# A half-sum on GpSimd ahead of VectorE's sum over one-hot products

## The chip, the cores and the metric

The kernel runs on one core of one Trainium2 chip. The metric is the device time of one execution in microseconds (us), lower is better. Times shown as a median are over separate runs; the profile is one further execution with the hardware profiler on.

## What is computed

One inference step of a decoder layer over 1024 prompt tokens and 64 sample tokens (8 sequences of 8), 1024 channels, all in float32. Two token mixers in parallel (retention and a gated linear recurrence) are merged and projected by `w_out`; behind them stands PEER, an expert retrieval by product keys, which is the part that matters here:

```python
q = (xf @ w_q).reshape(T, 8, 256)
s1 = einsum('thd,nd->thn', q[..., :128], k1)      # 128 scores each
s2 = einsum('thd,nd->thn', q[..., 128:], k2)
v1, i1 = top_k(s1, 16); v2, i2 = top_k(s2, 16)
cand = v1[..., :, None] + v2[..., None, :]        # 256 sums
sc, pidx = top_k(cand, 16)
expert = e1 * 128 + e2                            # of the 16 picks
act = gelu(einsum('td,tkd->tk', x, u_tab[expert]))
out = einsum('tk,tkd->td', softmax(sc) * act, v_tab[expert])
```

Each token has 8 heads of 16 picks: 128 rows of `u_tab`, each of 1024 numbers, are gathered and multiplied with the token.

## The kernel before, in words

**Tiles and units.** Tokens stand in 9 tiles of 128 (the last one is half full, and is turned so that 128 partitions hold its picks). A unit `m` is one head of a pair of tiles: 32 units of two tiles, then 4 units of one tile for the samples, 36 in all. VectorE makes a unit's picks in 16 pieces (`piece`, lines 1458 to 1530): the top 16 of each score row with `max`, `max_index` and `match_replace` (lines 1479 to 1487), 54 candidate sums (`pairs`, only those 54 of the 256 can be in the top 16), their top 16 with positions `bp` (lines 1497 to 1519), and the ids of the 54 candidates, `cid`. Piece 15 then compares an iota of 54 with each of the 16 positions (line 1528): `hot[128, tile, 16, 54]` has one 1 in each group of 54, and signals `pos_ready`.

**From positions to ids.** GpSimd multiplies `hot` with the 54 ids (`products`, line 1346), one instruction for each tile, and counts `hot_ready`. VectorE sums each group of 54 (`ids`, line 1438), which leaves the one id that was picked, and turns it into an integer (line 1440) for the gathers; `ids(m - 1)` is called in piece 8 of unit m, so half a unit later.

**The gathers and the dots.** GpSimd issues one indirect DMA for each of 1088 columns (`gather`, line 1354): 128 rows of `u_tab`, 512 KB, into one of six buffers (`rows`, `VD` = 6). Gather n waits until dot n - 6 is done (`used`). VectorE's `dot` (line 1540) waits for the landing, multiplies the 128 rows with the tokens and sums, one instruction and a short accumulator read. The products of a unit are put between gathers by `product_at`: behind gather `done[m] + 7` and `done[m] + 9` in most cases, where `done[m]` is the column at which piece 15 of unit m is done. On GpSimd's queue everything is in this one order.

**The last stage.** From 1639 us on the work goes by quarters (numbered -2 to 13, 32 batches each). In a batch VectorE builds a one-hot of the picks (line 1601) and its product with the weights in three bfloat16 parts (`oh1w`, line 1605), then does its pieces and two dots, laid out by `steps` from a table written by hand (`stages`). TensorE turns `oh1w` into expert weights W with 12 short matmuls (line 2016), and from quarter 0 on multiplies one block of the value table with W for each batch (line 2029, 16 instructions a batch, the float32 matmul being two). VectorE may run two batches ahead of TensorE. The value table streams in through four buffers (`vbuf`) on SyncE's queue beside the gathers. At the end of every fourth quarter VectorE adds the accumulators to the residual (`finish`, line 1619).

`Chain` (`gl_` for GpSimd) lets an instruction count a semaphore and has its own engine wait for that count before it goes on.

Of the kernel before, what the change touches and what calls it, by code (L numbers as in the profile page):

```python
# [23 lines left out]
ALU = mybir.AluOpType  # L24
ACT = mybir.ActivationFunctionType
AX = mybir.AxisListType.X

P = 128
# [16 lines left out]
TOPK = 16  # L45
# [8 lines left out]
NCAND = 54  # L54
# [142 lines left out]
def program(nc, I, O, S):  # L197
# [3 lines left out]
    def sem(name):  # L201
        return ctx.enter_context(nc.semaphore(name))

    def sb(c, name, shape, dt=F32):
        return c.enter_context(nc.sbuf_tensor(name, shape, dt))

    def bc(ap, axis, shape):
        return ap.unsqueeze(axis).broadcast_to(shape)
# [14 lines left out]
    def hold(eng):  # L223

        eng.sem_inc(hold_sem, 1)

    with ctx:
# [10 lines left out]
        gl_ = Chain(nc.gpsimd, pool_chain)  # L238
# [38 lines left out]
        cand, cid = sb(ctx, "cand", [P, 2, NCAND]), sb(ctx, "cid", [P, 2, NCAND])  # L277
        bp, bpf = sb(ctx, "bp", [P, 2, TOPK], U32), sb(ctx, "bpf", [P, 2, TOPK])
        hot = sb(ctx, "hot", [P, 2, TOPK, NCAND])
        eidf = sb(ctx, "eidf", [P, 2, TOPK])  # L280
# [95 lines left out]
        with nc.Block() as block:  # L376
            @block.sync
            def _(sp):
                def ada_load(i):
                    s = EARLY[i]  # L380
                    sp.dma_start(ada[i][:, :, :], I["w_ada"][:, s * ADA_W:(s + 1) * ADA_W].rearrange("(k p) n -> p k n", p=P)).then_inc(ada_in[i], 16)
                for dst, src in ((cT, "cT"), (vec, "vec"), (bada, "bada"), (ident, "ident")):
                    sp.dma_start(dst[:], I[src]).then_inc(small_in, 16)
                sp.dma_start(hnA[:, :, 0:TA], I["xT"][:, 0:TA].rearrange("(k p) t -> p k t", p=P)).then_inc(x_in[0], 16)
                ada_load(0)
                ada_load(1)
                sp.dma_start(hnB, I["xT"][:, TA:T].rearrange("(k p) t -> p k t", p=P)).then_inc(x_in[1], 16)
                ada_load(2)
                ada_load(3)
                w_in_load(sp, 0, 0)  # L390
                sp.wait_ge(ones_ready, 4)
                wab_load(sp, 0)
                for j in range(1, 6):
                    w_in_load(sp, 0, j)
                sp.wait_ge(act_done, 1)
                for dst, src in ((rope_c, "rope_c"), (rope_s, "rope_s"), (dmask, "dmask"), (smask, "smask"), (xi, "xi"),
                                 (zeta, "zeta"), (szeta, "szeta"), (gch, "gch"), (h0, "h0"), (c0, "c0"), (iota, "iota")):
                    sp.dma_start(dst[:], I[src]).then_inc(small_in, 16)
                s0_load(sp, 0)
                sp.wait_ge(mod_ps, len(EARLY))  # L400
                slab_load(sp, 0)
# [794 lines left out]
        tk, dk, pos_ready, hot_ready, idx_ready, max_ready, exp_ready = (sem(n) for n in ("tk", "dk", "pos_ready", "hot_ready", "idx_ready", "max_ready", "exp_ready"))  # L1196
# [16 lines left out]
        def unit(m):  # L1213

            if m < NGRP * H:
                return m // H, m % H, 2
            return NGRP, m - NGRP * H, 1

        def spilled(m):
            return m - H  # L1220

        def scored(m):

            return m if m < H else H + m - NGRP * H if m >= NGRP * H else m + NSU
# [18 lines left out]
        with nc.Block() as block:  # L1243
# [97 lines left out]
            @block.gpsimd  # L1341
            def _(g):
                def products(m, t):

                    g.wait_ge(pos_ready, m + 1)
                    g.tensor_tensor(hot[:, t, :, :], hot[:, t, :, :], bc(cid[:, t, :], 1, [P, TOPK, NCAND]), ALU.mult).then_inc(hot_ready, 1)  # L1346

                def gather(n, table, t, col):

                    s = n % VD  # L1350
                    if n >= VD:
                        g.wait_ge(used, n - VD + 1)
                    hold(g)
                    g.indirect_dma_start(rows[:, s, :], None, table[:, :], bass.IndirectOffsetOnAxis(ap=eidx[:, (t // 2) % 2, t % 2, col:col + 1], axis=0)).then_inc(landed[s], 16)  # L1354
                def reload(m):

                    j, n = spilled(m), unit(m)[2] * PW
                    if j >= 2:
                        g.wait_ge(tk, (m - 2) * TKU + 10)
                    at = scored(m) - H  # L1360
                    g.wait_ge(sp_out[at % 2], 16 * (at // 2 + 1))
                    g.dma_start(scr[:, m % 2, 0:n], S["sc"][j][:, 0:n]).then_inc(sc_in[m % 2], 16)

                def reload_at(m):

                    j = spilled(m)
                    return 2 * P - 1 if j < 2 else min(read[m - 2] + 8, done[m - 1] + 1)

                def product_at(m, x):

                    G, h, _ = unit(m)
                    at = min(done[m] + VD + 1 + 2 * x, read[m + 1] + VD - 2 if m + 1 < NUNIT else NU - 1)
                    return min(at, G * GT + h * TOPK - 1)
                for t in range(2):
                    products(0, t)
                for n in range(NU):
                    t = n // P
                    if n % TOPK == 0 and t % 2 == 0:
                        g.wait_ge(idx_ready, (t // 2) * H + (n % P) // TOPK + 1)
                    gather(n, I["peer_u"], t, n % P)  # L1380
                    for m in range(1, NUNIT):
                        if m + 1 >= H and m + 1 < NUNIT and n == reload_at(m + 1):
                            reload(m + 1)
                        for x in range(unit(m)[2]):
                            if n == product_at(m, x):
                                products(m, x)
                for n in range(NU, NU + TS):
                    gather(n, I["peer_v"], NT - 1, n - NU)

            @block.vector  # L1390
            def _(v):
# [42 lines left out]
                def ids(m):  # L1434

                    G, h, nt = unit(m)
                    v.wait_ge(hot_ready, 2 * m + 2 if m < NGRP * H else NGRP * H + m + 1)
                    v.tensor_reduce(eidf[:, 0:nt, :], hot[:, 0:nt, :, :], AX, ALU.add).then_inc(dk, 1)  # L1438
                    v.wait_ge(dk, m + 1)
                    v.tensor_copy(eidx[:, G % 2, 0:nt, h * TOPK:(h + 1) * TOPK], eidf[:, 0:nt, :]).then_inc(idx_ready, 1)  # L1440

# [16 lines left out]
                def piece(x):  # L1458
# [7 lines left out]
                    if p < 10:  # L1466
# [5 lines left out]
                        if p == 8 and m and m != H:  # L1472
                            ids(m - 1)
# [177 lines left out]
                for half in range(2):  # L1651
                    if half:
                        ids(H - 1)
                    slots = steps(plan[2 + half])
                    for f in range(half * H // 2, (half + 1) * H // 2):
                        mix_vector(v, zB, f, lambda: mixed_step(next(slots)))
# [16 lines left out]
                for row in plan[7:]:  # L1673
                    i = row[0]
                    g, q = divmod(i, 4)
                    quarter(row)
                    if i >= 0 and q == 3:
                        finish(g)
                    if i == 10:
                        ids(NUNIT - 1)  # L1680
                    if i == 11:
                        soft_high(NGRP)
                        tile_weights(NT - 1, TS).then_inc(ef_ready, 1)
                        v.wait_ge(ef_ready, NT)
                    if i == 12:
                        dl_(v.tensor_tensor(sel, ident[:, 0:TS], ident[:, TS:P], ALU.add))
                        v.wait_ge(used, NU + TS)
                        v.sem_inc(acc_ready, 1)
                    if i >= 0 and i < 12 and q == 0:
                        soft_high(g + 1)  # L1690
                        tile_picks(2 * g + 2)
                    if i >= 0 and i < 12 and q == 2:
                        tile_picks(2 * g + 3)
                        if g:
                            norm(g - 1)
# [488 lines left out]
```

## Time and profile before

| | |
|---|---|
| time, median of 3 runs | 4003.32 us (4001.05 to 4008.05) |
| profiled execution: its time | 3999.14 us |
| profiled execution: its span | 3997.3 us (1.84 us lie around it) |
| busy: TensorE, VectorE, ScalarE, GpSimd | 3684.9, 2830.9, 1557.9, 1603.1 us |
| granted TensorE clock, mean | 0.971 of full speed |
| chain that ended last, by engine | PE 36%, DVE 28%, DMA 9%, issue 7% |

PE is TensorE, DVE is VectorE, ACT is ScalarE and POOL is GpSimd. A duration in a row of groups is the mean of one instruction; in a row by source it is min/median/max in ns. An idle time in square brackets stands in front of the instruction and names what ended it. A record's length holds the time in which the instruction was started but could not go on.

### The profile page before, as it was taken

The numbers are of one execution on the slowest core, as the hardware profiler recorded it, in microseconds if no ns is written. First come the engines' busy times: TensorE is split into PE (matmuls) and PEld (weight loads), VectorE is DVE, ScalarE is ACT, GpSimd is POOL, SyncE is SP. The second block draws the span as 40 slices with busy tenths as digits, with TensorE's granted clock in tenths as the row PEclk, the third lists the DMA queues.
The fourth block names the chain that finished last, engine by engine and source line by source line (L and its number), as shares of the span: only waits on it lengthen the run. The fifth ranks groups of instructions, "written<-read, shape, count | busy, mean of one in ns | idle before, by whom it ended". The sixth has DMA issues, their size and how long they took to land.

```text
span 3997.3 us, 65568 instructions
## 1 busy us (share of the span) xinstructions
PE 3684.9 (92%) x21008; PEld 2903.7 (73%) x21008; DVE 2830.9 (71%) x6544; ACT 1557.9 (39%) x3678; POOL 1603.1 (40%) x1252
## 2 busy tenths in 40 slices
PE   7999969999999988878899899999899999899998
PEld 4665656666656657767787788888788887788887
DVE  3333427588877767889899999999998898683000
ACT  3222211111112211676555455555555655465200
POOL 0000003243233324435666566666667776471000
PEclk9999989999999989999999999999999999999999
DMA  7343334565466578778999999999999999995443
GB/s 236 106 124 103 100 133 153 154 188 181 162 199 202 175 244 290 260 242 319 389 374 371 330 398 375 372 385 396 360 374 390 398 406 352 371 381 189 140 159 126
DMA packets 415882, 1060.14 MB, mean 265 GB/s; under 512 B 39665, under 2 KB 171121, under 8 KB 415729
## 3 DMA queue, kind: packets, MB, share of 16 engines
q0 software_dynamic: 168000, 610.87, 41.5%
q1 hardware_dynamic: 242672, 437.10, 31.1%
q10 hardware_dynamic: 5056, 10.49, 0.7%
q8 instruction: 52, 0.85, 0.1%
q14 instruction: 102, 0.83, 0.1%
HBM read 1031.70 MB, written 26.62 MB: 265 GB/s over the span
## 4 chain that ended last, share of the span: by engine, by line
PE 36%; DVE 28%; DMA 9%; issue 7%; POOL 2%; PEld 1%; ACT 0%; DVEq 0%; ACTq 0%; SPq 0%; PEldq 0%; POOLq 0%
DVE rows L1540 16%; PE vacc L2029 13%; PE vacc L783 10%; DMA rows<-in_peer_u,eidx 7%; PE vacc L752 4%; PE scat L1963 3%; DVE oh L1601 2%; POOL rows L1354 2%; DVE oh1w L1605 1%; DMA vbuf<-in_peer_v 1%; DVE eidf L1438 1%; PEld vacc L2029 1%; DVE hot L1528 1%; PE scat L2016 1%; PE vacc L606 1%
## 5 line engine op out<-in xcount | busy, mean ns | idle before, releaser
L2029 PE MATMUL vacc<-W,vbuf 128*128 (+1 forms) x8192 | 1900.4, 387 | 27.1 <-DMA vbuf<-in_peer_v 18.2
L1354 POOL DMA_INDIRECT rows<-in_peer_u,eidx x1088 | 1362.7, 1252 | 1270.4 <-DVE dots L1540 874.1
L2029 PEld LDWEIGHTS vacc<-W,vbuf 128*128 128x128 f32 x8192 | 1537.2, 192 | 224.4 <-issue 26.6
L1540 DVE CUSTOM_DVE_ANT_0 rows<-rows,htok 128x1024 f32<-128x1024 f32 x1088 | 1349.0, 1265 | 75.3 <-DMA rows<-in_peer_u,eidx 66.9
L1794 ACT ACTIVATE dist<-iota,e2s 128x128 bf16<-128x128 f32 x2048 | 648.6, 391 | 18.0 <-DVE wpart L1579 15.7
L1801 ACT ACTIVATE W<-scat 128x256 f32 x448 | 171.6, 383 | 813.4 <-PE scat L2016 806.1
L783 PE MATMUL vacc<-W 128*128 128x384 f32 x1280 | 431.3, 491 | 3.5 <-PE vacc L783 2.3
L1346 POOL TENSOR_TENSOR hot<-hot,cid 128x864 f32<-128x864 f32 x68 | 133.4, 1965 | 668.6 <-DVE hot L1528 667.4
L1797 ACT ACTIVATE oh<-dist,ones 128x512 bf16<-128x512 bf16 x512 | 369.6, 722 | 16.7
L783 PEld LDWEIGHTS vacc<-W 128*128 128x128 f32 x1280 | 240.0, 191 | 168.8 <-issue 10.7
L2016 PEld LDWEIGHTS scat<-oh1w,oh 128*128 128x128 bf16 x5376 | 217.9, 97 | 127.2 <-issue 69.7
L1605 DVE TENSOR_TENSOR oh1w<-oh,wpart 128x768 bf16<-128x768 bf16 x512 | 287.8, 562 | 17.7
L2016 PE MATMUL scat<-oh1w,oh 128*128 128x64 bf16 x5376 | 234.0, 192 | 50.3 <-DVE oh1w L1605 46.7
L1601 DVE TENSOR_TENSOR oh<-iota,e1s 128x256 bf16<-128x256 bf16 x512 | 165.4, 323 | 134.2 <-PE scat L2016 122.3
L1963 PE MATMUL scat<-W 128*128 128x256 f32 (+1 forms) x1024 | 250.4, 400 | 10.4 <-DVE W L1423 8.2
L1963 PEld LDWEIGHTS scat<-W 128*128 128x128 f32 x1024 | 195.0, 195 | 49.6 <-issue 9.7
L783 PE MATMUL vacc<-rows,W 128*128 128x320 f32 x640 | 181.9, 437 | 4.9 <-ACTq L683 2.5
L752 PE MATMUL vacc<-W 128*128 128x256 f32 x768 | 170.3, 382 | 2.8 <-PE vacc L793 2.8
L219 ACT ACTIVATE W<-vacc 128x768 f32<-128x768 f32 x32 | 25.9, 810 | 374.5 <-PE vacc L783 374.5
L752 PEld LDWEIGHTS vacc<-W 128*128 128x128 f32 x768 | 146.4, 191 | 28.4 <-issue 7.1
L783 PEld LDWEIGHTS vacc<-rows,W 128*128 128x128 f32 x640 | 118.4, 190 | 57.4 <-issue 7.8
L1354 POOL DMA_INDIRECT rows<-in_peer_v,eidx x64 | 90.1, 1408 | 42.2 <-DVE htok L1549 21.7
(300 smaller groups left out, 2913.5 us busy)
## 6 DMA issues: line engine op xcount, KB each, us to landing
vbuf<-in_peer_v SPq DMA_DIRECT2D x512, 512.0 KB
W<-in_w_in SPq DMA_DIRECT2D x80, 512.0 KB, 5.5
W<-in_wq SPq DMA_DIRECT2D x64, 512.0 KB, 4.7
vbuf<-in_w_ada SPq DMA_DIRECT2D x9, 2048.0 KB, 8.0
rows<-in_peer_u,eidx POOLq DMA_INDIRECT x1088, 7.9
W<-in_w_in SPq DMA_DIRECT2D x16, 1024.0 KB, 5.6
W<-in_w_out SPq DMA_DIRECT2D x2, 4096.0 KB, 19.8
W<-in_w_ada SPq DMA_DIRECT2D x3, 2048.0 KB, 16.1
```

What stands on the lines that cost most here:

```text
L752: mm = pe.matmul(dst, z.hnT[:, k, t * P:(t + 1) * P], w_qkv[:, k, :], start=(k == 0), stop=(k == KC - 1))
L783: mm = pe.matmul(pslice(z, pj if bank == "pj" else pk, s), w_part[j - 1][:, k, :], z.hnT[:, k, lo:hi], start=(k == 0), stop=(k == KC - 1))
L1354: g.indirect_dma_start(rows[:, s, :], None, table[:, :], bass.IndirectOffsetOnAxis(ap=eidx[:, (t // 2) % 2, t % 2, col:col + 1], axis=0)). ...
L1540: v.tensor_tensor_reduce(rows[:, s, :], rows[:, s, :], htok[:, t % 2, :], 1.0, 0.0, ALU.mult, ALU.add, dots[t % 3][:, c:c + 1]).then_inc(u ...
L1601: v.tensor_tensor(oh1[:, h, :, :, :], bc(iota4[:, half * HK:(half + 1) * HK, :], 1, shp), bc(e1s[:, k].rearrange("p (a n) -> p a n", n=2), ...
L1605: v.tensor_tensor(oh1w[:, h, :, :, :, :], bc(oh1[:, h, :, :, :], 1, shp), bc(wpart[:, u * QB + j, :, :, :], 3, shp), ALU.mult).then_inc(oh ...
L1794: ins = act.activation(dist[:, n, :], iota[:, :], ACT.Abs, bias=e2s[:, bass.ds(k, 1)], scale=-1.0)
L1797: act.activation(oh2[:, h, :, :], dist[:, :, :], ACT.Relu, bias=ones[:, 0:1], scale=-1.0).then_inc(oh2_ready, 1)
L1801: act.activation(W[:, half * HK:(half + 1) * HK, bass.ds(i * (VB * SB) + (u * P + q * SB), SB)], banks[q % 2][:, 0:SB * HK].rearrange("p ( ...
L1963: mm = pe.matmul(scat[u][:, 0:n], wq[j % 4][:, k, :], hn2T[g][:, k, 0:n], start=(k == 0), stop=(k == KC - 1))
L2016: mm = pe.matmul(banks[h][:, n * HK:(n + 1) * HK], oh2[:, h, n, :], oh1w[:, h, j, n // 2, :, n % 2], start=(j == 0), stop=(j == 2), skip_g ...
L2029: mm = pe.matmul(vacc[:, k, :], vbuf[:, s, k * P:(k + 1) * P], W[:, e1, :].rearrange("p o t -> p (o t)"), start=(clear and s == 0 and k % ...
```

## The change

`products` adds a second instruction on GpSimd: after the multiplication (now followed by a wait of GpSimd for its own result) the upper 27 of each 54 products are added onto the lower 27. VectorE's sum reads only those 27 of each group. `hot_ready` counts once for each tile as before.

```diff
@@ products (GpSimd)
                     g.wait_ge(pos_ready, m + 1)
-                    g.tensor_tensor(hot[:, t, :, :], hot[:, t, :, :], bc(cid[:, t, :], 1, [P, TOPK, NCAND]), ALU.mult).then_inc(hot_ready, 1)
+                    half = NCAND // 2
+                    gl_(g.tensor_tensor(hot[:, t, :, :], hot[:, t, :, :], bc(cid[:, t, :], 1, [P, TOPK, NCAND]), ALU.mult))
+                    g.tensor_tensor(hot[:, t, :, 0:half], hot[:, t, :, 0:half], hot[:, t, :, half:], ALU.add).then_inc(hot_ready, 1)
@@ ids (VectorE)
                     v.wait_ge(hot_ready, 2 * m + 2 if m < NGRP * H else NGRP * H + m + 1)
-                    v.tensor_reduce(eidf[:, 0:nt, :], hot[:, 0:nt, :, :], AX, ALU.add).then_inc(dk, 1)
+                    v.tensor_reduce(eidf[:, 0:nt, :], hot[:, 0:nt, :, 0:NCAND // 2], AX, ALU.add).then_inc(dk, 1)
```

## Rows read from the trace of the kernel before

**Rows 1.** The page's first part: busy time, share of the span, instructions.
```profile
PE 3684.9 (92%) x21008; PEld 2903.7 (73%) x21008; DVE 2830.9 (71%) x6544; ACT 1557.9 (39%) x3678; POOL 1603.1 (40%) x1252
```

**Rows 2.** Busy time by stretch: start:end, length, engines, clock, DMA share, GB/s.
```profile
1639.00:1997.00 358.00, 294.43 (x2346) 253.85 (x2347) 324.57 (x862) 242.48 (x644) 187.98 (x148) 0.98 0.86 309
1997.00:2961.00 964.00, 900.06 (x6302) 771.27 (x6301) 933.06 (x2375) 516.57 (x1351) 616.20 (x493) 0.98 0.97 373
2961.00:3356.00 395.00, 384.01 (x2717) 332.70 (x2715) 348.01 (x780) 229.66 (x593) 283.96 (x199) 0.99 0.98 387
```

**Rows 3.** Waits from 1997 to 2961 us: total, times, longest.
```profile
DVE rows L1540 <- DMA rows<-in_peer_u,eidx: 6.4, 11, 1.9
...
PE scat L2016 <- DVE oh1w L1605: 36.2, 31, 4.4
```

**Rows 4.** VectorE's waits from 2961 to 3356 us.
```profile
DVE rows L1540 <- DMA rows<-in_peer_u,eidx: 34.6, 65, 1.5
DVE eidf L1438 <- POOL hot L1346: 4.0, 1, 4.0
```

**Rows 5.** By source line: count, min/median/max ns, first and last start us, forms.
```profile
L1438 DVE TENSOR_REDUCE eidf<-hot x36: 1043/1944/1953, 636.9 to 3345.0; 128x32 f32<-128x1728 f32 x32, 128x16 f32<-128x864 f32 x4
...
L1346 POOL TENSOR_TENSOR hot<-hot,cid x68: 1847/1882/2295, 631.5 to 3343.1; 128x864 f32<-128x864 f32 x68
...
L1540 DVE CUSTOM_DVE_ANT_0 rows<-rows,htok x1088: 1197/1218/3485, 676.5 to 3488.4; 128x1024 f32<-128x1024 f32 x182
```

**Rows 6.** GpSimd's timeline, 2228 to 2240 us: start, length, line, operation.
```profile
2228.93 2.11 POOL L1346 TENSOR_TENSOR hot<-hot,cid 128x864 f32<-128x864 f32 x1
2231.20 1.78 POOL L1354 DMA_INDIRECT rows<-in_peer_u,eidx  x1 [0.16 <-issue]
...
2234.23 1.89 POOL L1346 TENSOR_TENSOR hot<-hot,cid 128x864 f32<-128x864 f32 x1
2238.04 1.17 POOL L1354 DMA_INDIRECT rows<-in_peer_u,eidx  x1 [1.92 <-DVE dots L1540]
```

**Rows 7.** VectorE's timeline over the same stretch.
```profile
2228.12 1.20 DVE L1540 CUSTOM_DVE_ANT_0 rows<-rows,htok 128x1024 f32<-128x1024 f32 x1
...
2229.25 2.88 DVE L1540 CUSTOM_DVE_ANT_0 rows<-rows,htok 128x1024 f32<-128x1024 f32 x1
...
2232.06 0.28 DVE L1601 TENSOR_TENSOR oh<-iota,e1s 128x256 bf16<-128x256 bf16 x1
...
2234.01 3.21 DVE L1540 CUSTOM_DVE_ANT_0 rows<-rows,htok 128x1024 f32<-128x1024 f32 x1
```

**Rows 8.** VectorE's timeline: the first and the last stalled instruction after 1639 us.
```profile
1647.43 1.95 DVE L1601 TENSOR_TENSOR oh<-iota,e1s 128x256 bf16<-128x256 bf16 x1
...
3279.23 2.60 DVE L1540 CUSTOM_DVE_ANT_0 rows<-rows,htok 128x1024 f32<-128x1024 f32 x1 [0.21 <-DMA rows<-in_peer_u,eidx]
```

**Rows 9.** GpSimd's timeline at 1597 us: two products back to back.
```profile
1597.71 3.67 POOL L1346 TENSOR_TENSOR hot<-hot,cid 128x864 f32<-128x864 f32 x2 [8.81 <-DVE hot L1528]
```

**Rows 10.** VectorE's timeline beside it: an instruction with one input.
```profile
1597.54 0.48 DVE L1479 MAX8 tv<-scr 128x8 f32<-128x128 f32 x2
```

**Rows 11.** GpSimd's products (line 1346) by stretch: busy us and count.
```profile
1639.00:1997.00 358.00, 25.97 (x13) 0.98 0.86 309
1997.00:2961.00 964.00, 60.05 (x30) 0.98 0.97 373
2961.00:3356.00 395.00, 10.14 (x5) 0.99 0.98 387
```

**Rows 12.** VectorE's sums (line 1438) by stretch: busy us and count.
```profile
1639.00:1997.00 358.00, 11.66 (x6) 0.98 0.86 309
1997.00:2961.00 964.00, 29.17 (x15) 0.98 0.97 373
2961.00:3356.00 395.00, 6.13 (x5) 0.99 0.98 387
```

**Rows 13.** GpSimd's shortest arithmetic instruction, from the groups of 0 to 3 us.
```profile
L2172 POOL MEMSET const-uint8-127<- 128x1 uint8 x1 | 0.1, 118 | 0.0
```

## The prediction

> **What bounds the kernel now.** I read the page's busy line first, then busy time by stretch, then the waits of the stretch in which the change works, then single products in the timeline of both engines. The page calls TensorE the busiest engine, 92% of the span against 71% for VectorE and 40% for GpSimd [rows 1]. By that average a microsecond on VectorE would be cheap and one on GpSimd free. The stretches say otherwise. From 1997 to 2961 us VectorE is busy 933.06 of 964 us, 97% [rows 2], and TensorE waits 36.2 us in 31 pieces for VectorE's weighted one-hots, while VectorE's largest wait is 6.4 us, for gathered rows [rows 3]. So VectorE sets the pace there, with TensorE close behind (900.06 us): time added on VectorE counts in full, time removed soon meets TensorE. From 1639 to 1997 us VectorE is busy 324.57 of 358 us, also the fullest engine. From 2961 to 3356 us TensorE is busy 384.01 of 395 us, and VectorE waits 34.6 us for gathers [rows 2, 4]: here small changes on VectorE are largely swallowed. Before 1639 us units overlap the mixers and queries, where TensorE's work makes the chain, and after 3356 us no unit is left; I carry both over unchanged.
>
> **What a GpSimd product costs VectorE today.** This is the reading on which all hangs. A dot takes 1.218 us in the median [rows 5]. At 2228.93 GpSimd starts a product of 2.11 us [rows 6]; the dot that was already running ends normally (1.20 us), but the one behind it, started at 2229.25, takes 2.88 us, 1.66 too long. The next product, 1.89 us from 2234.23, meets a dot that takes 3.21 us, 1.99 too long [rows 7]. The pattern repeats: going through all 48 products between 1639 and 3356 us [rows 11] against VectorE's records, I find 44 that stretch a VectorE instruction by more than 1.1 us, nearly always by 1.65 to 2.3. The first of them is a one-hot of 1.95 us that otherwise takes 0.28, the last a dot of 2.60 us [rows 8, 7]. The stretched ones are dots, comparisons, products and casts. Instructions that read one tensor of scores are not stretched: two products back to back at 1597.71 run for 3.67 us [rows 9] over `max` instructions of their usual length (0.48 us for two) [rows 10]. So while GpSimd does such an instruction, a VectorE instruction with two inputs in SBUF stands still. Moving arithmetic from VectorE to GpSimd is then no relief: its time on GpSimd comes back on VectorE.
>
> The Trainium skill ("SBUF — State Buffer", Who interferes with whom) has this as a rule against this change: VectorE and GpSimd share a port pair under an exclusive lock, taken for a whole instruction, and an instruction with two SBUF inputs contends with a GpSimd instruction that reads SBUF. The trace agrees, with 44 of 48 products. The rule charges the whole instruction where I take from the rows what a stalled record shows; with 0.94 us for each of 44 additions the sum below would be 4.8 us higher, 4024 us.
>
> **What is removed.** The sum over 1728 numbers takes 1.944 us, the one over 864 takes 1.043 [rows 5], so a two-tile unit saves 1.944 - 1.043 = 0.90 us (both rows read dense groups; the groups of 27 now stand 54 apart, which I cost at nothing, and rival (d) carries the doubt). A one-tile unit goes from 864 to 432 numbers, by the same slope 0.45 us less. It is one serial instruction on VectorE with nothing beside it on that engine, so it counts wherever VectorE is the bound. Counts [rows 12], where the third stretch has 1 two-tile and 4 one-tile units: 6 x 0.90 = 5.4 us, 15 x 0.90 = 13.5 us, 0.90 + 4 x 0.45 = 2.7 us. Together 21.6 us.
>
> **What is added.** Each of the 68 products is followed by an addition of 432 numbers in 128 partitions. No GpSimd row has that size. A product of 864 takes 1.882 us [rows 5], and GpSimd's shortest arithmetic instruction 0.118 us [rows 13]; so the fixed part is at most about 0.1 us, and 432 numbers should take 0.94 to 1.0 us. The bounds, by the nearest rows, are 0.118 us (all fixed, nothing per number) and 1.882 us (no gain from halving). I take half a product, as the operation and the kinds of operands are the same.
>
> What does an addition cost VectorE? GpSimd first waits for its own product; gaps on its queue are 0.16 us [rows 6]. In that gap the VectorE instruction that stood still gets going, so the addition waits until it is over, as products do when a dot already runs, and then holds up the next one. In the example this is the one-hot of line 1601, which has two inputs too. A product of 864 stretches it by 1.66 us at the least, half of that is 0.83, which I take. The ends: 0, if the additions find only one-input instructions beside them, and 1.9, the whole of the largest addition above. Counts of colliding products: 12 of 13, 28 of 30, 4 of 5 (the rest of the 48 fell on one-input work, on idle time, or on instructions that read PSUM). That makes 12 x 0.83 = 10.0 us, 28 x 0.83 = 23.2 us, 4 x 0.83 = 3.3 us.
>
> **Sum.** First stretch 10.0 - 5.4 = +4.6 us; second 23.2 - 13.5 = +9.7 us; third 3.3 - 2.7 = +0.6 us. VectorE's last sum already waits 4.0 us for its product [rows 4], and nothing covers that: the picks of the last tiles stand behind it. The addition makes this wait about 1 us longer, +1.0. Total +15.9 us, on the profiled execution 3999.1 + 15.9 = 4015 us. The median of the runs lies 4.2 us above that execution, so the forecast is 4003.3 + 15.9 = 4019 us.
>
> **What is queued behind the new wait.** On GpSimd's queue the gathers come behind each product. The gather at 2231.20 moves by 0.16 + about 1.0 of waiting for VectorE + 0.94, some 2 us, against the 0.83 by which VectorE itself slips. It refills the buffer of a dot that ended at 2229.2, and six dots lie before its use, some 12 us, so it has room. At 2238.04 GpSimd is waiting for VectorE again, after 1.92 us of idle time [rows 6]; two additions of 2 us each less VectorE's own 1.7 take nearly all of that. I cost the gathers at nothing where VectorE is dense, because this idle time hides the delay. If the cover is gone, the rows come up to 1 us late for each addition. SyncE's queue is not touched; its value stream waits for TensorE alone.
>
> **Rivals.**
> (a) The gathers come late. For it: VectorE waits for rows already, 6.4 and 34.6 us [rows 3, 4], and GpSimd's cover is used up by my own count. Against: 6.4 us in 964 is little, and in the last stretch TensorE is the bound. Price 1 us for each of 44 colliding additions over the sum: 4019 + 44 = 4063 us at worst, about 4040 when half of them are late.
> (b) Additions are cheap for VectorE. If an addition finds one-input work (`max`, `max_index`, `match_replace`) in half of the cases, 18 of 36.5 us go: 15.9 - 18 = -2, so 4001 us, no change. For it: such instructions stood unharmed beside products at 1597 us. Against: most stalls are in a run of dot, dot, one-hot, weighted one-hot, all of them with two inputs.
> (c) The other side: faster. The place is the gap behind each product from 1639 to 2961 us: if the port is given to VectorE first and additions run only beside one-input work or idle time, then nothing of the 33.2 us is added and 18.9 are saved, 4003.3 - 18.9 = 3984 us, less where TensorE takes over. It decides from the point where an addition costs VectorE less than (21.6 - 1.0) / 44 = 0.47 us. Against it stand 44 stalls of a whole product.
> (d) The change doesn't do what it says: the sum over groups of 27 with gaps is no shorter than 1.944 us. Then 21.6 us less are saved and it ends at 4041.
>
> **How the numbers follow.** A measurement of this kernel tells about 0.2%, 8 us, from no change, so "same" is 3995 to 4011. The forecast (+10 to +28) has 0.70, (a) 0.11, (b) 0.12, (c) 0.05, (d) 0.02. An addition at 0.7 us instead of 0.83 gives 30.8 - 21.6 + 1 = +10, at 1.1 us 48.4 - 21.6 + 1 = +28; with late gathers on half of the additions it reaches +38. The range 4006 to 4041 leaves out the far end of (a) and most of (b) and (c). Slower: 0.70 + 0.11 + 0.02 less the 0.03 of the forecast that may fall short, 0.80. Same: 0.12 + 0.03, 0.15. Faster: 0.05.
>
> **What the profile after would show.** The sum of line 1438 at 1.04 us for two tiles; 68 additions on GpSimd near 0.95 us alone and up to 2 us where they wait; behind each product a normal VectorE instruction and then one stretched by 0.8 to 1.0 us; VectorE's busy time up by some 15 us with fewer numbers read; the stretch from 1997 to 2961 us longer by about 10 us; the wait for gathered rows nearly unchanged. The prediction is wrong if the additions show beside VectorE instructions of normal length, if waits for gathered rows grow by more than 10 us, or if TensorE's wait for weighted one-hots does not grow.

## The result and the profile after

The changed kernel takes 4028.6 us (median of 4 runs, 4021.1 to 4030.6) against 4004.35 us (4 runs, 4001.05 to 4008.05): 24 us slower, ratio 1.0057 with a 95% interval of 1.0045 to 1.0069. Forecast was 4019 us in a range of 4006 to 4041, that is +16 us. The direction and the stalls hold; what was said of the saving and of the gathers does not, and the size is too small by a third. The profiled execution took 4027.7 us, its span is 4025.9, 28.6 us longer than before.

The changed kernel's groups by source line (columns as in [rows 5]); the product is now line 1347, the addition 1348, the sum 1440, the dot 1542:
```profile
L1347 POOL TENSOR_TENSOR hot<-hot,cid x68: 1851/1883/2834, 632.1 to 3373.9; 128x864 f32<-128x864 f32 x68
...
L1348 POOL TENSOR_TENSOR hot<-hot x68: 1105/1120/2453, 634.0 to 3375.8; 128x432 f32<-128x432 f32 x68
...
L1440 DVE TENSOR_REDUCE eidf<-hot x36: 593/1044/1054, 638.2 to 3377.0; 128x32 f32<-128x864 f32 x32, 128x16 f32<-128x432 f32 x4
```
The sum over 27 of each 54 numbers takes 1.044 us, as a dense one of that size did [rows 5]: the gaps cost nothing. The addition takes 1.12 us where nothing is in its way, not 0.94 to 1.0. If the product and the addition cost the same for each number, 1.883 us for 864 and 1.120 for 432 lie on a line of 1.77 ns a number and 0.36 us fixed; run 1 below shows that the form of the operands matters, too.

The stretches of the changed kernel, cut at the same quarters (columns as in [rows 2]):
```profile
1642.00:2004.00 362.00, 299.35 (x2348) 257.24 (x2348) 329.08 (x861) 243.42 (x647) 207.42 (x161) 0.96 0.85 306
2004.00:2989.00 985.00, 913.01 (x6304) 780.33 (x6303) 945.58 (x2376) 517.29 (x1352) 719.16 (x523) 0.97 0.95 365
2989.00:3387.00 398.00, 384.88 (x2716) 333.25 (x2714) 352.88 (x779) 229.57 (x592) 277.75 (x205) 0.98 0.98 385
```
Against [rows 2] they are 4, 21 and 3 us longer, where I had 4.6, 9.7 and 1.6. The first quarter begins 3 us later and what stands behind the last stretch is some 3 us shorter. So the dense stretch (1997 to 2961 us before) carries the miss. VectorE's busy time there is up by 12.5 us (945.58 against 933.06), near what I worked out. The other part is waiting:

VectorE's and TensorE's waits from 2004 to 2989 us (to be laid beside [rows 3]):
```profile
DVE rows L1542 <- DMA rows<-in_peer_u,eidx: 17.8, 24, 2.1
...
PE scat L2018 <- DVE oh1w L1607: 42.4, 34, 4.3
```
The wait for gathered rows went from 6.4 to 17.8 us. Over the whole span, before and then after:
```profile
DVE rows L1540 <- DMA rows<-in_peer_u,eidx: 66.9, 110, 4.4
```
```profile
DVE rows L1542 <- DMA rows<-in_peer_u,eidx: 81.9, 145, 4.1
```

VectorE's and GpSimd's timelines around the products of the unit shown in [rows 6, 7]:
```profile
2241.17 2.88 DVE L1542 CUSTOM_DVE_ANT_0 rows<-rows,htok 128x1024 f32<-128x1024 f32 x1
...
2243.98 1.18 DVE L1603 TENSOR_TENSOR oh<-iota,e1s 128x256 bf16<-128x256 bf16 x1
...
2246.83 3.54 DVE L1542 CUSTOM_DVE_ANT_0 rows<-rows,htok 128x1024 f32<-128x1024 f32 x1
...
2250.31 2.12 DVE L1542 CUSTOM_DVE_ANT_0 rows<-rows,htok 128x1024 f32<-128x1024 f32 x1
```
```profile
2240.85 2.12 POOL L1347 TENSOR_TENSOR hot<-hot,cid 128x864 f32<-128x864 f32 x1
2243.05 1.97 POOL L1348 TENSOR_TENSOR hot<-hot 128x432 f32<-128x432 f32 x1
...
2247.41 1.88 POOL L1347 TENSOR_TENSOR hot<-hot,cid 128x864 f32<-128x864 f32 x1
2249.36 1.99 POOL L1348 TENSOR_TENSOR hot<-hot 128x432 f32<-128x432 f32 x1
```
It is the picture that was forecast. The products stretch a dot by 1.66 and one by 2.33 us; the addition waits for this dot (1.97 us instead of 1.12) and then stretches the next instruction, here a one-hot from 0.28 to 1.18 us and a dot from 1.22 to 2.12, each by 0.90 us. Where the next one is a weighted one-hot of 0.56 us, it takes 1.42, 0.86 more.

### The profile page after: what moved, and what is told of

The parts are those of the page before. It is cut to its first block, busy times and chain, and to the rows that moved or that the text cites. A ratio compares the mean times of both kernels' runs of the same rounds, so it can differ in the third digit from the quotient of the medians.

```text
span 4025.9 us, 65636 instructions
## 1 busy us (share of the span) xinstructions
PE 3702.3 (92%) x21008; PEld 2915.7 (72%) x21008; DVE 2846.2 (71%) x6544; ACT 1559.1 (39%) x3678; POOL 1756.0 (44%) x1320
## 4 chain that ended last, share of the span: by engine, by line
PE 36%; DVE 24%; DMA 12%; issue 8%; POOL 3%; PEld 1%; ACT 0%; DVEq 0%; ACTq 0%; SPq 0%; PEldq 0%; POOLq 0%
PE vacc L2031 13%; DVE rows L1542 12%; DMA rows<-in_peer_u,eidx 10%; PE vacc L783 10%; PE vacc L752 4%; PE scat L1965 3%; POOL rows L1356 3%; DVE oh L1603 2%; DVE oh1w L1607 1%; DMA vbuf<-in_peer_v 1%; PEld vacc L2031 1%; DVE hot L1530 1%; PE scat L2018 1%; PE vacc L606 1%; PE vacc L793 1%
## 5 line engine op out<-in xcount | busy, mean ns | idle before, releaser
L2031 PE MATMUL vacc<-W,vbuf 128*128 (+1 forms) x8192 | 1914.5, 389 | 24.3 <-DMA vbuf<-in_peer_v 16.0
L1356 POOL DMA_INDIRECT rows<-in_peer_u,eidx x1088 | 1411.3, 1297 | 1148.0 <-DVE dots L1542 757.4
L1542 DVE CUSTOM_DVE_ANT_0 rows<-rows,htok 128x1024 f32<-128x1024 f32 x1088 | 1350.2, 1265 | 90.9 <-DMA rows<-in_peer_u,eidx 81.9
L1607 DVE TENSOR_TENSOR oh1w<-oh,wpart 128x768 bf16<-128x768 bf16 x512 | 303.4, 593 | 17.6
L1603 DVE TENSOR_TENSOR oh<-iota,e1s 128x256 bf16<-128x256 bf16 x512 | 191.2, 373 | 127.7 <-PE scat L2018 116.5
```

What stands on the lines that cost most here:

```text
L1542: v.tensor_tensor_reduce(rows[:, s, :], rows[:, s, :], htok[:, t % 2, :], 1.0, 0.0, ALU.mult, ALU.add, dots[t % 3][:, c:c + 1]).then_inc(u ...
L1603: v.tensor_tensor(oh1[:, h, :, :, :], bc(iota4[:, half * HK:(half + 1) * HK, :], 1, shp), bc(e1s[:, k].rearrange("p (a n) -> p a n", n=2), ...
L1607: v.tensor_tensor(oh1w[:, h, :, :, :, :], bc(oh1[:, h, :, :, :], 1, shp), bc(wpart[:, u * QB + j, :, :, :], 3, shp), ALU.mult).then_inc(oh ...
L2031: mm = pe.matmul(vacc[:, k, :], vbuf[:, s, k * P:(k + 1) * P], W[:, e1, :].rearrange("p o t -> p (o t)"), start=(clear and s == 0 and k % ...
```

## The experiments

Theory S: GpSimd's instructions come back on VectorE as stalls, and the sum is what I wrote. Rivals: the addition is harmless and the shorter sum is at fault (F); the gathers come late (G, the prediction's (a)), with its own cause open: GpSimd's queue, or the DMA engines. Each kernel was timed beside the kernel before, whose median was then between 3999.7 and 4004.4 us; differences are taken to that median. A ratio stands with its 95% interval; 0.0017 to either side is 7 us.

**1. The added work alone.** GpSimd's second instruction has the same size, but multiplies with ones and leaves the data as they are, and VectorE sums 54 as before.
```diff
-                    g.tensor_tensor(hot[:, t, :, :], hot[:, t, :, :], bc(cid[:, t, :], 1, [P, TOPK, NCAND]), ALU.mult).then_inc(hot_ready, 1)
+                    half = NCAND // 2
+                    low = hot[:, t, :, 0:half]
+                    gl_(g.tensor_tensor(hot[:, t, :, :], hot[:, t, :, :], bc(cid[:, t, :], 1, [P, TOPK, NCAND]), ALU.mult))
+                    g.tensor_tensor(low, low, bc(ones[:, 0:half], 1, [P, TOPK, half]), ALU.mult).then_inc(hot_ready, 1)
```


> GpSimd does a second instruction of 432 numbers behind each product (the lower half times ones, so nothing changes in the data), and VectorE still sums 54. Theory S (GpSimd's time comes back on VectorE, 0.88 us for each of 44 instructions, plus late gathers and late products): the whole cost of the change without its saving, 4004 + 42 to 46, so 4046 to 4050 us. Rival F (the addition is nearly free and the loss lies in the shorter sum over groups with gaps): 4004 to 4010 us.


Measured: 4038.9 us against 4001.8, +37.1 us, ratio 1.0096 (1.0079 to 1.0113). F falls. S put it at 42 to 46, a little high; the prediction's own terms, 36.5 us of stalls and 1.0 for the last sum, gave 37.5. The second instruction in this kernel:
```profile
L1349 POOL TENSOR_TENSOR hot<-hot,ones x68: 1033/1039/2380, 632.0 to 3384.2; 128x432 f32<-128x432 f32 x68
```
It is 0.08 us shorter than the addition (1.120 us), and where it stretches VectorE it mostly costs 0.78 to 0.83 us instead of 0.86 to 0.90. So this run is some 3 to 4 us lighter than the cost of the real addition (an estimate, 46 times 0.08), and a part of its "a little high" is that.

**2. The short sum alone.** VectorE reads 27 of 54, GpSimd adds nothing. (Picks in the upper half then gather row 0; what that changes in their transfers was not looked at.)
```diff
-                    v.tensor_reduce(eidf[:, 0:nt, :], hot[:, 0:nt, :, :], AX, ALU.add).then_inc(dk, 1)
+                    v.tensor_reduce(eidf[:, 0:nt, :], hot[:, 0:nt, :, 0:NCAND // 2], AX, ALU.add).then_inc(dk, 1)
```


> VectorE sums 27 of each 54 products and nothing is added on GpSimd; picks in the upper half then get id 0 (left out: their ids; 1088 gathers of 512 KB remain). Theory S: 21.6 us of VectorE's time go, TensorE takes over in part, 4004 - 12 to - 20, so 3984 to 3992 us. Rival F (the short sum saves nothing): 4000 to 4006 us. The two runs together must give the change: their differences to the kernel before should sum to +24 within 6 us.


Measured: 3988.75 us, -13.1 us, ratio 0.9967 (0.9955 to 0.9978). VectorE's busy time fell by 26.6 us over the span (2830.9 to 2804.3), and 21.6 of savings lie in the late stages by the prediction's count; 13.1 arrived. VectorE's wait for rows rose instead, from 66.9 us to:
```profile
DVE rows L1540 <- DMA rows<-in_peer_u,eidx: 77.1, 126, 4.1
```
In the dense quarters VectorE's busy time is 13 us down and the time 6 us; 4.3 us went into waits for rows and 2.2 into waits for TensorE. So TensorE took a part as well. The kernel of run 1 waits 72.0 us for rows. The two totals add up: 37.1 - 13.1 = +24.0 us, the change has +24.3. The stretches do not add up as well: in the dense one +20.6 and -5.6 us stand against the change's +20.4, and the rest cancels elsewhere. In total the cost was forecast well and the saving was not.

**3. The addition moved behind the next gather**, so that GpSimd doesn't wait for its product ahead of a gather.
```diff
...
+                def halves(m, t):
...
                     half = NCAND // 2
+                    g.wait_ge(pool_chain, gl_.base + made.index((m, t)) + 1)
                     g.tensor_tensor(hot[:, t, :, 0:half], hot[:, t, :, 0:half], hot[:, t, :, half:], ALU.add).then_inc(hot_ready, 1)
...
-                            if n == product_at(m, x):
+                            if n == product_at(m, x)[0]:
                                 products(m, x)
+                            if n == product_at(m, x)[1]:
+                                halves(m, x)
```


> The changed kernel with each addition put behind the next gather instead of directly behind its product, so that GpSimd no longer waits for its own result ahead of a gather. Theory S (0.88 us of stall for each addition): these stay, 44 x 0.88 - 21.6 = +17 of the +24 us. Theory G (the rest of the loss, 11 us between 1997 and 2961 us, is gathers held up behind product, wait and addition in one block): waits for gathered rows fall from 82 back to 67 to 72 us and the time to 4012 to 4020 us. If the block is not what makes them late: 4025 to 4031 us.


Measured: 4058.4 us, +56.6 us, ratio 1.0142 (1.0125 to 1.0159), so 32 us more than the change itself: a clear miss of all that was expected. Waits for rows are 76.4 us in all against 81.9, but VectorE's busy time rose by 31 us over the changed kernel (2877.6 against 2846.2). GpSimd's and VectorE's timelines of this kernel at one addition (line 1355), which stands right behind a gather of 1.78 us:
```profile
2255.28 1.11 POOL L1355 TENSOR_TENSOR hot<-hot 128x432 f32<-128x432 f32 x1
```
```profile
2254.34 0.28 DVE L1614 TENSOR_TENSOR oh<-iota,e1s 128x256 bf16<-128x256 bf16 x1
2254.66 2.16 DVE L1618 TENSOR_TENSOR oh1w<-oh,wpart 128x768 bf16<-128x768 bf16 x1
```
The same addition now costs 1.60 us: the weighted one-hot began 0.62 us ahead of the addition's record, would have been over before it, and still stood through all of it. Between 2149 and 3027 us this repeats for all 28 additions. The profile calls GpSimd's spans rough, so whether the addition took hold of VectorE before its record or the record begins late stays open; the cost on VectorE does not depend on it. So the price of one GpSimd instruction depends on what stands on VectorE in the 0.6 us ahead of it. Right behind its product, where VectorE has an instruction waiting to go first, is the cheaper place here (0.86 to 0.90 us).

**4. The product moved to VectorE too**, from the kernel before; GpSimd issues gathers alone.
```diff
@@ GpSimd's queue: both places that call products are gone
-                            if n == product_at(m, x):
-                                products(m, x)
...
@@ ids (VectorE)
-                    v.wait_ge(hot_ready, 2 * m + 2 if m < NGRP * H else NGRP * H + m + 1)
+                    v.wait_ge(pos_ready, m + 1)
+                    v.tensor_tensor(hot[:, 0:nt, :, :], hot[:, 0:nt, :, :], bc(cid[:, 0:nt, :], 2, [P, nt, TOPK, NCAND]), ALU.mult).then_inc(dk, 1)
+                    v.wait_ge(dk, 2 * m + 1)
                     v.tensor_reduce(eidf[:, 0:nt, :], hot[:, 0:nt, :, :], AX, ALU.add).then_inc(dk, 1)
```


> From the kernel before: the product too moves to VectorE (one instruction of 1728 numbers for two tiles, ahead of the sum), and GpSimd only issues gathers. Theory S: VectorE gains 66 stalls of 1.3 us in the mean, 87 us in its records, of which 75 lie between 1639 and 3356 us, and pays 21 x 1.95 + 4 x 1.05 = 45 us there; the difference of 30 us shows where VectorE is the bound, so 3972 to 3985 us. Rival (VectorE is relieved by what GpSimd does): 32 x 1.95 + 4 x 1.05 = 67 us more on VectorE, 4045 to 4065 us.


Measured: 3975.5 us (3971.6 to 3979.1), -26.4 us, ratio 0.9937 (0.9921 to 0.9954): faster than both kernels by giving VectorE more work. The groups of this kernel (line, operation, shapes, count, busy, mean):
```profile
L1537 DVE CUSTOM_DVE_ANT_0 rows<-rows,htok 128x1024 f32<-128x1024 f32 x1088 | 1299.6, 1218 | 82.3 <-DMA rows<-in_peer_u,eidx 66.9 <-issue 5.5 <-DVE W L1062 1.5
...
L1433 DVE TENSOR_TENSOR hot<-hot,cid 128x1728 f32<-128x1728 f32 x32 | 62.5, 1952 | 0.3
```
The mean dot is 1.218 us, exactly the median of [rows 5]; no stretched one is left. VectorE does 32 products more of 1.95 us, and its busy time still fell from 2830.9 to 2813.6 us. Earlier gathers are not the cause of it: VectorE waits 66.9 us for rows, as before. The last sum's wait of 4.0 us for its product [rows 4] is gone. With the 17.3 us of busy time that is 21 of the profile's 26.9 us; the rest is not traced.

**5. The same pair with a lighter value stream.** To see whether late rows swallow the saving, half of each value block was left out (after the first four blocks; the expert outputs of the other channels are then wrong), in four kernels: before, changed, short sum alone, added work alone.
```diff
...
-                            sp.dma_start(vbuf[:, s, :], I["peer_v"][bass.ds((i * VB + s) * P, P), :]).then_inc(v_in[s], 16)
+                            sp.dma_start(vbuf[:, s, 0:D // 2], I["peer_v"][bass.ds((i * VB + s) * P, P), 0:D // 2]).then_inc(v_in[s], 16)
```


> The kernel before with half of each value block loaded (after the first four blocks only columns 0 to 511 of 1024; the expert outputs of the other channels are then wrong), so the value stream moves 256 KB instead of 512 KB beside the gathers. It is half of a pair. Theory B (gathered rows come late because both streams share the DMA engines, busy 0.97): waits for gathered rows fall from 67 to under 20 us and the time to 3940 to 3975 us. Rival L (they are late through the ring of six buffers and GpSimd's queue alone): waits stay over 55 us, 3990 to 4005 us.

> The changed kernel with the same half of the value blocks left out. Theory B: with rows always in time the full saving of the short sum shows, and the pair differs by what VectorE's own stalls and savings give, 44 x 0.88 - 21.6 + 1 = +18 us or, with TensorE closer as the bound, less; waits for rows under 25 us in both. Rival L: the difference stays at +22 to +27 us and waits for rows are again some 15 us longer than in the other half of the pair.


Measured: 3962.7 us (ratio to the kernel before 0.9907, 0.9890 to 0.9923) and 3977.7 us (0.9945, 0.9928 to 0.9961). The change now costs 15.0 us instead of 24.3. VectorE's waits for rows in the thin kernel before, over the span:
```profile
DVE rows L1545 <- DMA rows<-in_peer_u,eidx: 20.8, 22, 4.2
```
and in the thin changed kernel:
```profile
DVE rows L1547 <- DMA rows<-in_peer_u,eidx: 22.0, 28, 4.2
```
They hardly differ, against 66.9 and 81.9 us with the full stream. In the dense stretch the median time from a gather's issue to its landing fell from 8.0 to 6.1 us in the kernel before.

> The run with the short sum alone (ids of the upper half are left out), with half of each value block left out as in the thin pair. Measured so far: the short sum alone gains 13 us with the full value stream, where its own durations promise 21.6. Theory B (the rest went into waits for rows, because both streams share the DMA engines): against the thin kernel before (3963 us) now 18 to 22 us, so 3941 to 3945 us, waits for rows under 25 us. Rival T (TensorE takes over, whatever the gathers do): again 11 to 14 us, 3949 to 3952 us, and VectorE's wait for TensorE's batches grows by the rest.

> GpSimd's second instruction alone (VectorE sums 54), with half of each value block left out. Theory B: with rows in time the cost is the stalls alone, 44 x 0.88 + 1.2 = 40 us over the thin kernel before, minus what waits for TensorE swallow after 2961 us (4 x 0.88): 36 to 40 us, so 3999 to 4003 us. If the thin streams also hid a part of GpSimd's lateness that the full stream shows, less than 35 us.


Measured: 3943.4 and 4000.8 us. Against the kernel before as timed beside each they are 58.3 and 0.9 us faster, the thin kernel before 37.0 us. That is a saving of 21.3 us and a cost of 36.1 us; taken straight from the medians, which were not timed side by side, 19.3 and 38.1. The first two add up to 14.8 us, against 15.0 for the changed kernel. So the saving rose from 13.1 to about 20, where theory B had 18 to 22 and rival T 11 to 14, and the cost stayed about where it was (37.1). The intervals are 7 us to either side, so the rise of the saving is not clear of noise by the times alone; the waits carry it: the short sum raises VectorE's wait for rows by 10.2 us with the full stream (66.9 to 77.1) and by nothing with the thin one (20.8 to 20.6), and its waits for TensorE's batches stay (152.8 and 154.7 us), which rival T had growing. From quarter 8 to 10 the short sum saves nothing in either pair (0.1 and 0.5 us, where the sum had 2.7): there VectorE waits 32 us for rows with the full stream and 29 for TensorE with the thin one.

**6. What kind of GpSimd instruction does it.** Behind each addition of the changed kernel one more instruction on the upper 432 numbers, which nobody reads again: a copy onto themselves, or zeros.
```diff
-                    g.tensor_tensor(hot[:, t, :, 0:half], hot[:, t, :, 0:half], hot[:, t, :, half:], ALU.add).then_inc(hot_ready, 1)
+                    gl_(g.tensor_tensor(hot[:, t, :, 0:half], hot[:, t, :, 0:half], hot[:, t, :, half:], ALU.add))
+                    up = hot[:, t, :, half:]
+                    g.tensor_copy(up, up).then_inc(hot_ready, 1)       # the one kernel
+                    g.memset(up, 0.0).then_inc(hot_ready, 1)           # the other
```


> The changed kernel with one more GpSimd instruction behind each addition: a copy of the upper 432 numbers onto themselves, one input from SBUF. Theory P (any GpSimd instruction that reads SBUF holds the pair of ports against VectorE's two-input instructions): a third stretched VectorE instruction behind each product, 44 x (its length less 0.2 us), so with 0.6 to 0.7 us some 18 to 22 us more than the changed kernel, 4046 to 4052 us. Rival Q (only GpSimd's two-input instructions do it): no third stretched instruction, 4029 to 4036 us.

> As the run with the copy, but the extra instruction writes zeros into the upper 432 numbers and reads nothing. Theory P: GpSimd's time alone, no stretched dot, comparison or product beside it; at most 8 us over the changed kernel through later gathers, 4029 to 4037 us. Rival R (every GpSimd instruction stops VectorE): as with the copy, 4040 us or more.


The kernel with the copy (line 1350), GpSimd and then VectorE:
```profile
2250.20 0.55 POOL L1350 COPY hot<-hot 128x432 f32<-128x432 f32 x1
```
```profile
2249.10 1.18 DVE L1605 TENSOR_TENSOR oh<-iota,e1s 128x256 bf16<-128x256 bf16 x1
2250.32 0.84 DVE L1609 TENSOR_TENSOR oh1w<-oh,wpart 128x768 bf16<-128x768 bf16 x1
```
The kernel with the zeros at the same place:
```profile
2246.80 0.47 POOL L1350 MEMSET hot<- 128x432 f32 x1
```
```profile
2245.70 1.18 DVE L1605 TENSOR_TENSOR oh<-iota,e1s 128x256 bf16<-128x256 bf16 x1
2246.92 0.56 DVE L1609 TENSOR_TENSOR oh1w<-oh,wpart 128x768 bf16<-128x768 bf16 x1
```
The copy, one input, stretches a weighted one-hot that begins beside it from 0.56 to 0.84 us, in all 16 such places after 1639 us. In the other kernel it takes 0.56 us beside the memset, here and in all 15 such places from 2143 us on. So a write alone doesn't stop this two-input instruction, a read does, with one input as with two. This is the rule of the Trainium skill ("SBUF — State Buffer", Who interferes with whom): with two inputs in SBUF, VectorE contends with a GpSimd instruction that reads SBUF, not with one that only writes; the traces agree, 0.84 against 0.56 us.

Two inputs are not the whole condition on VectorE's side. In the trace of before, two casts of 128x128 numbers, with one input each, begin half a microsecond ahead of a product and take 2.62 us together, where the same pair takes 0.56 us in the kernel of run 4:
```profile
2544.64 1.85 POOL L1346 TENSOR_TENSOR hot<-hot,cid 128x864 f32<-128x864 f32 x1
```
```profile
2544.11 2.62 DVE L1565 CAST ef<-ef 128x128 f32<-128x128 uint32 x2
```
And beside the zeros a cast with one input (line 1583) takes 0.42 us instead of 0.23, at 2293.89 and again at 2850.18 us. No run here tells which one-input instructions are open to this and which, as `max`, are not.

The times were a surprise: 4054.7 us with the copy (+55.0, ratio 1.0144, 1.0127 to 1.0161) and 4046.4 with the zeros (+46.7, ratio 1.0122, 1.0105 to 1.0139). Both lie outside what was expected, and by its time alone the kernel with the zeros would have spoken for rival R; it is the trace that rules R out. The copy costs 8 us more than the zeros, with 6.3 us more busy time on VectorE (2855.5 against 2849.2): that is what its read adds. The zeros thus cost 22 us more than the changed kernel has, where I allowed 8, with only 3.0 us more busy time on VectorE (2849.2 against 2846.2). VectorE's waits in the kernel with the zeros, over the span:
```profile
DVE rows L1544 <- DMA rows<-in_peer_u,eidx: 90.9, 139, 4.1
DVE eidf L1442 <- POOL hot L1350: 18.1, 7, 5.7
```
Waits for rows are up by 9.0 us over the changed kernel (81.9) and waits for the products by 5.7 (12.4). Waits for TensorE moved as well (116.5 to 122.3 us), so the span's sum is no proof by itself. The stretches are clearer: from quarter 1 to 10 this kernel is 15 us longer than the changed one in their profiles, its waits for rows there are 13.6 us longer (26.1 against 17.8 and 36.2 against 30.9), and VectorE's busy time grows by 1.6. So GpSimd's time costs also where it hardly stretches VectorE: 68 instructions of 0.47 us and a wait each push back the gathers and the products behind them.

## Why the prediction was right, and where not

- **What bounds.** Right. From 1997 to 2961 us VectorE set the pace, and work added to it counted: in run 1 these quarters are 20.6 us longer, where the sum had 23.2 of stalls. That run 1 meets the sum so closely in total (37.1 us for 36.5 of stalls and 1.0 of waiting) is in part luck. In its profile the three stretches are 8.3, 20.6 and 5.7 us longer, the start before the first quarter 5.7 us longer and the part behind the last stretch 3.5 us shorter; the prediction carried both ends over unchanged. By the page's averages the addition on GpSimd, busy 40%, would have been free.
- **The stalls.** Right in kind and nearly in size: of the 48 additions from 1639 us on, 46 stretch a VectorE instruction, 43 of them by 0.85 to 0.92 us against the 0.83 taken, 39.6 us in all against 36.5. The addition takes 1.12 us instead of 0.94 to 1.0. The fixed part is not bounded by the 0.118 us of the smallest memset: a tiny instruction of another kind was a bad bound. A product with ones over 432 numbers (1.039 us, run 1) leaves about 0.2 us fixed, the addition of two halves about 0.36, both estimates from two rows each. The place behind the product kept the stall near the estimate; run 3 shows 1.60 us for the same addition elsewhere. That only instructions with two inputs stand still is too narrow; the prediction's own list has casts in it.
- **The short sum.** Each saves 0.90 us, as said, and the gaps cost nothing. The step that failed is "it counts wherever VectorE is the bound", 21.6 us together. Measured alone it is 13.1 us. Runs 2 and 5 show what took most of the rest: with the full value stream rows land 8.0 us after their issue in the median, and a VectorE that is early waits for them (10.2 us more in run 2, nothing more with the thin stream). With the changed kernel's stalls in place the saving vanishes in the dense stretch: run 1 and the changed kernel both take 985 us from quarter 1 to 7, and the wait for rows there is 8.7 us in the first and 17.8 in the second. With half of the value stream the change costs 15.0 us, where the sum said 15.9; by stretches its profile has 0.1, 12.8 and 3.3 us against 4.6, 9.7 and 1.6, so that closeness is in part luck again.
- **The gathers at nothing.** This is for two thirds the same failed step from the other side: of the 15 us by which the waits for rows grew, the short sum alone brings 10.2 (run 2), the added work alone 5.1 (run 1). I saw 1.92 us of idle time on GpSimd as cover and noted that it was nearly used up, and still priced the rest at zero. My own test for being wrong, waits for rows up by more than 10 us, came true: 66.9 to 81.9 us. Rival (a) was a part of the truth and not an alternative; its price, 44 us, was too high: the waits grew by 15 us.
- **The last sum.** It waited 5.2 us instead of 4.0 [rows 4], +1.2 against +1.0. Not foreseen were six other waits of the sum for its products, 12.4 us in all with this one, five of them before 1110 us. The changed kernel reaches the first quarter 3.1 us later than before; the short sum alone does so, too (3.2 us), and run 1 even more (5.7 us), so what this start is due to stays open.
- **Rivals (b), (c), (d)** fell: 46 of 48 additions stretched something, two (at 1748.74 and 3375.85 us) did not, and the sum over 27 took 1.044 us.

## What to carry to other kernels

Before moving elementwise work from a full VectorE to an idle GpSimd, look at VectorE's records beside what GpSimd does today: where dots of 1.22 us read 2.9 and 3.2, GpSimd's arithmetic is already paid for on VectorE. In run 4 VectorE took over 67 us of products and was still busy 17 us less, so 84 us of stretch went away: 1.43 ns for each of the 68 x 864 numbers, against 1.13 when VectorE does the product itself (1.952 us for 1728). Here the gain lay in moving it back (26 us). Cost and saving on the same engine need not be worth the same: here nearly all of the cost came through, the saving only until the next supplier, the gathered rows, was late. When a queue also issues gathers, look at what an instruction put on it does to them: here they came later even behind an instruction that hardly stretched VectorE.

## What was not expected of the hardware

- A GpSimd instruction that reads SBUF stopped VectorE instructions whose records began up to 0.62 us before its own (GpSimd's records are rough). An addition of 1.11 us then costs 1.60 us, against 0.90 behind a VectorE instruction that goes first. In the trace of before the same shows at dots that began 0.22 us ahead of a product (1.99 us too long [rows 7]).
- A memset on GpSimd (0.47 us for 432 numbers) left weighted one-hots beside it at 0.56 us, a copy of the same numbers (0.55 us) stretched them to 0.84.
- 68 memsets still cost 22 us by the medians (18 in the profiles), most of it through gathers and products that came later; VectorE's busy time grew by 3.0 us. The few stretches found beside them, of 0.2 us, are casts with one input.
- Halving the value stream shortened a gather's landing from 8.0 to 6.1 us in the median, at a DMA share of 0.90 instead of 0.97 in the dense stretch.
